# Hybrid two-layer encoder trunk on one core: load order, parameter transfers, first spread and last store

## What is computed

```python
def rms_norm(x, g):
    y = x * lax.rsqrt(jnp.mean(x * x, axis=-1, keepdims=True) + EPS)
    return y * g

x = x + rglru_sgu_mixer(rms_norm(x, norm_ab), w_in_ab, ..., w_out_ab)      # layer 0
#   z = h @ w_in; a_x, a_g, b_u, b_v = split(z, 4)
#   y_a = rg_lru(causal_dwconv(a_x)) * gelu(a_g)
#   y_b = spatial_gating(gelu(b_u), gelu(b_v)); concat(y_a, y_b) @ w_out
x = x + conv_ffn(rms_norm(x, norm_ffn[0]), ...)
x = x + chunk_band_attention(rms_norm(x, norm_attn), w_qkv, rel_bias, w_o)  # layer 1
x = x + conv_ffn(rms_norm(x, norm_ffn[1]), ...)
return rms_norm(x, norm_final)
```

## Time and profile before

| | us |
|---|---|
| median of 3 runs | 1108.13 |
| lowest and highest | 1107.46, 1108.34 |
| the profiled execution | 1108.31 |
| its span, first to last instruction | 1106.4 |
| PE busy in the span | 1094.4 |
| granted TensorE clock, mean | 0.997 |

### The profile page before, as it was taken

The page is one execution under the profiler, slowest core; times in us unless marked ns, Lnnn a source line. Parts: engine busy times, 40 slices in busy tenths (PEclk is TensorE's granted clock), DMA queues, the critical chain, the costliest instruction groups (busy, mean ns, idle before and its releaser), DMA issues.

```text
span 1106.4 us, 15451 instructions
## 1 busy us (share of the span) xinstructions
PE 1094.4 (99%) x5167; PEld 911.4 (82%) x5167; DVE 650.8 (59%) x1068; ACT 436.8 (39%) x672; POOL 530.2 (48%) x415
## 2 busy tenths in 40 slices
PE   8999999999999999999999999999999999999997
PEld 6888888888888888888888888888888888888886
DVE  6777557766666632223877677676766666651113
ACT  6783433322222232334656455453323232233222
POOL 5568645444444445554332323364544444455552
PEclk9999999999999999999999999999999999999998
DMA  8273323222222232333322222132222222223212
GB/s 308 91 240 114 113 78 115 95 95 95 95 95 95 95 114 96 114 108 110 105 92 80 81 91 77 57 114 96 95 100 96 104 98 95 95 95 110 98 39 77
DMA packets 37875, 115.07 MB, mean 104 GB/s; under 512 B 4912, under 2 KB 7600, under 8 KB 37840
## 3 DMA queue, kind: packets, MB, share of 16 engines
q1 hardware_dynamic: 34976, 109.86, 29.6%
q10 hardware_dynamic: 2864, 4.74, 1.3%
HBM read 112.19 MB, written 6.59 MB: 107 GB/s over the span
## 4 chain that ended last, share of the span: by engine, by line
PE 90%; DVE 0%; ACT 0%; DVEq 0%; issue 0%
PE bank L1252 28%; PE bank L1253 28%; PE bank L1254 28%; PE bank L1560 2%; PE bank L1543 2%; PE bank L1572 1%; PE bank L1570 1%; PE bank L1466 0%; PE bank L1465 0%; PE bank L1554 0%; DVE x L1245 0%; PE bank L1291 0%; PE bank L1298 0%; PE bank L1512 0%; PE bank L1504 0%; PE bank L1520 0%
## 5 line engine op out<-in xcount | busy, mean ns | idle before, releaser
L381 POOL TENSOR_TENSOR wl<-raw,wh 128x512 fp32r<-128x512 f32 x190 | 250.1, 1316 | 546.3 <-ACT wh L477 546.3
L1252 PE MATMUL bank<-xh,wh 128*128 128x512 f32 x976 | 382.7, 392 | 2.3 <-DVE xl L859 2.3
L1254 PE MATMUL bank<-xh,wl 128*128 128x512 f32 x976 | 380.2, 390 | 0.0
L1253 PE MATMUL bank<-xl,wh 128*128 128x512 f32 x976 | 380.1, 389 | 0.0
L477 ACT ACTIVATE wh<-raw 128x1024 fp32r<-128x1024 f32 x190 | 201.1, 1061 | 356.0 <-PE bank L1254 313.4
L383 POOL TENSOR_TENSOR wl<-raw,wh 128x512 fp32r<-128x512 f32 x190 | 259.5, 1366 | 0.0
L1252 PEld LDWEIGHTS bank<-xh,wh 128*128 128x128 f32 x976 | 183.2, 188 | 41.8 <-issue 2.1
L1254 PEld LDWEIGHTS bank<-xh,wl 128*128 128x128 f32 x976 | 183.2, 188 | 38.4
L1253 PEld LDWEIGHTS bank<-xl,wh 128*128 128x128 f32 x976 | 183.3, 188 | 36.9
L1252 PE MATMUL bank<-ah,wh 128*128 128x512 f32 (+1 forms) x357 | 134.6, 377 | 0.0
L1253 PE MATMUL bank<-al,wh 128*128 128x512 f32 (+1 forms) x357 | 134.4, 377 | 0.0
(11 more groups left out here) (208 smaller groups left out, 1148.2 us busy)
## 6 DMA issues: line engine op xcount, KB each, us to landing
raw<-weights SPq DMA_DIRECT2D x190, 512.0 KB, 3.2
bias_scratch<-ext_scratch SPq DMA_DIRECT2D x1, 4096.0 KB, 18.2
bias<-bias_scratch ACTq DMA_DIRECT2D x8, 512.0 KB, 3.6
x<-x_in SPq DMA_DIRECT2D x8, 256.0 KB, 5.8
out<-x SPq DMA_DIRECT2D x4, 384.0 KB, 2.9
raw<-weights SPq DMA_DIRECT2D x4, 256.0 KB, 5.7
out<-x ACTq DMA_DIRECT2D x2, 256.0 KB, 2.8
lng<-ln_g SPq DMA_DIRECT2D x1, 256.0 KB, 8.5
```

Source lines behind the costliest of these rows:

```text
L381: nc.gpsimd.tensor_tensor(low[:, 0:FIRST], raw[:, c % RAW, 0:FIRST], high[:, 0:FIRST], ALU.subtract).then_inc(w_half, 1)
L1252: nc.tensor.matmul(dst, w_hi_part, m_hi, start=first, stop=False)
L1253: nc.tensor.matmul(dst, w_hi_part, m_lo, start=False, stop=False)
L1254: return nc.tensor.matmul(dst, w_lo_part, m_hi, start=False, stop=last)
```

## The change

Six things are changed.

1. SP no longer issues the gains. The recurrence's parameters are moved to stand behind the gains, and ACT issues both in one transfer (`par[:, 0:C_FFN]`, now 72 columns, semaphore `gains_in`). DVE's first step on `lam` and ACT's first `xh` wait for it.
2. SP issues x tile 0 first, then the first half of unit 0, x tiles 1 to 3, the second half, x tiles 4 and 5, and then as before. ACT takes x tile 0, first half, x tiles 1 to 3, second half, x tiles 4 and 5, and then as before.
3. ACT's table load for Sqrt moves from in front of the first half to behind the split of unit 4, in front of the root.
4. POOL makes the low parts of the second halves of units 0 and 1 in two pieces of 128x256 also. PE waits for the first piece before k 4, and for the second before k 6.
5. PE does k 0 of unit 3 before `spread_rstd(0)`, with its wait for the unit's low part in front.
6. SP's last store of three tiles is cut into one of two tiles and one of one tile.

```diff
+OUT_PARTS = [[(2, 5), (5, 8)], [(2, 5), (5, 7), (7, 8)]]
+C_LRU = C_GAIN + N_NORMS * KT
+C_FFN = C_LRU + MT_A * 8
...
-            sp.dma_start(par[:, 0:C_FFN], params[:, 0:C_FFN]).then_inc(gains_in, 16)
...
+            load_x(0)
             load_half(0, 0)
-            for m in range(3):
+            for m in range(1, 4):
                 load_x(m)
             load_half(0, 1)
-            for m in range(3, 6):
+            for m in range(4, 6):
                 load_x(m)
...
-                for n in range(2):
-                    tiles_out = slice(OUT_POOL + 3 * n, OUT_POOL + 3 * n + 3)
-                    sp.wait_ge(out_dve, 6 * half + 3 * n + 3)
+                for first, last in OUT_PARTS[half]:
+                    tiles_out = slice(first, last)
+                    sp.wait_ge(out_dve, (KT - OUT_POOL) * half + last - OUT_POOL)
                     sp.dma_start(out[:, tiles_out, cols], x[:, tiles_out, cols]).then_inc(out_done, 16)
...
                 pool.wait_ge(w_hi, c + 1)
-                nc.gpsimd.tensor_tensor(low[:, FIRST:], raw[:, c, FIRST:], high[:, FIRST:], ALU.subtract
-                                        ).then_inc(w_lo, 1)
+                for n, part in enumerate((slice(FIRST, FIRST + FIRST // 2), slice(FIRST + FIRST // 2, UNIT))):
+                    nc.gpsimd.tensor_tensor(low[:, part], raw[:, c, part], high[:, part], ALU.subtract
+                                            ).then_inc(w_lo if n else half_lo, 1)
...
-            act.dma_start(par[:, C_LRU:], params[:, C_LRU:]).then_inc(lru_in, 16)
+            act.dma_start(par[:, 0:C_FFN], params[:, 0:C_FFN]).then_inc(gains_in, 16)
...
-            preload(ACT.Sqrt, 1)
+            act.wait_ge(gains_in, 16)
+            first_hi(0)
             half_hi_part(0)
...
             split_hi(3)
             split_hi(4)
+            preload(ACT.Sqrt, 1)
             statistics(0)
...
+            pe.wait_ge(w_lo, U_AX + 4)
+            tiles(bank[MIX_BANKS[3]][:], U_AX + 3, range(1), True, False, (xh, xl))
             spread_rstd(0)
-            whole(U_AX + 3, MIX_BANKS[3])
+            tiles(bank[MIX_BANKS[3]][:], U_AX + 3, range(1, KT), False, True, (xh, xl)).then_inc(w_used, 1)
```

More of the change, by code:

```diff
@@ L59 @@
 OUT_POOL = 2
-C_FFN = C_GAIN + N_NORMS * KT
+OUT_PARTS = [[(2, 5), (5, 8)], [(2, 5), (5, 7), (7, 8)]]
+C_LRU = C_GAIN + N_NORMS * KT
+C_FFN = C_LRU + MT_A * 8
 FFN_COLS = FF_KT * 8
-C_LRU = C_FFN + 2 * FFN_COLS
-N_PARAMS = C_LRU + MT_A * 8
+N_PARAMS = C_FFN + 2 * FFN_COLS
 EXT = T + P
@@ L229, in trunk @@
         half_in = [sem(f"half_in{i}") for i in range(2)]
-        half_hi, half_lo, warm_ready, lru_in = (sem(n) for n in ("half_hi", "half_lo", "warm_ready", "lru_in"))
+        half_hi, half_lo, warm_ready = (sem(n) for n in ("half_hi", "half_lo", "warm_ready"))
         gains_in, lam_series, rate_done = sem("gains_in"), sem("lam_series"), sem("rate_done")
@@ L331, in _ @@
             load_unit(2)
-            sp.dma_start(par[:, C_FFN:C_LRU], params[:, C_FFN:C_LRU]).then_inc(par_in, 16)
+            sp.dma_start(par[:, C_FFN:], params[:, C_FFN:]).then_inc(par_in, 16)
             for c in range(3, RAW):
@@ L361, in _ @@
                 cols = slice(HALF * half, HALF * half + HALF)
-                for n in range(2):
-                    tiles_out = slice(OUT_POOL + 3 * n, OUT_POOL + 3 * n + 3)
-                    sp.wait_ge(out_dve, 6 * half + 3 * n + 3)
+                for first, last in OUT_PARTS[half]:
+                    tiles_out = slice(first, last)
+                    sp.wait_ge(out_dve, (KT - OUT_POOL) * half + last - OUT_POOL)
                     sp.dma_start(out[:, tiles_out, cols], x[:, tiles_out, cols]).then_inc(out_done, 16)
-            sp.wait_ge(out_done, 16 * 6)
+            sp.wait_ge(out_done, 16 * 7)
         @block.gpsimd
@@ L532, in _ @@
             nc.scalar.activation(ln_tmp, ln_var, ACT.Exp, scale=-1.0).then_inc(lam_exp, 1)
-            preload(ACT.Sqrt, 1)
+            act.wait_ge(gains_in, 16)
+            first_hi(0)
             half_hi_part(0)
-            act.wait_ge(gains_in, 16)
-            for m in range(3):
+            for m in range(1, 4):
                 first_hi(m)
             other_half_hi(0)
-            for m in range(3, 6):
+            for m in range(4, 6):
                 first_hi(m)
@@ L896, in _ @@
             num, den, ratio2, series = ln_tmp, ln_rstd, ln_var, bank[LAM_BANK][:, 0:4]
-            dve.wait_ge(lru_in, 16)
+            dve.wait_ge(gains_in, 16)
             link(ts(lru_rate, lam, -1.0, None, ALU.mult))
@@ L1307, in _ @@
             for unit, k in FIRST_TILES:
-                if k in (0, 2):
-                    pe.wait_ge(half_lo, 2 * unit + 1 + k // 2)
-                if k == FIRST // P:
+                if k in (0, 2, 4):
+                    pe.wait_ge(half_lo, 3 * unit + 1 + k // 2)
+                if k == 6:
                     pe.wait_ge(w_lo, unit + 1)
@@ L1697, in pack_params @@
     cols = [n.reshape(KT, P).T for n in norms]
+    lru = np.concatenate([lru_conv_w, lru_conv_b[None], r_b[None], i_b[None], lam[None]], 0)
+    cols.append(lru.reshape(8, MT_A, P).transpose(2, 1, 0).reshape(P, 8 * MT_A))
     for layer in range(2):
@@ L1704, in pack_params @@
         cols += [tail, np.zeros((P, 4), tail.dtype)]
-    lru = np.concatenate([lru_conv_w, lru_conv_b[None], r_b[None], i_b[None], lam[None]], 0)
-    cols.append(lru.reshape(8, MT_A, P).transpose(2, 1, 0).reshape(P, 8 * MT_A))
     return np.concatenate(cols, 1)
```

## The result

The changed kernel takes 1109.50 us (median of 21 runs, 1108.36 to 1110.72), the kernel before 1108.19 (21 runs, 1107.46 to 1109.11). The ratio is 1.0013, 95% interval 1.0007 to 1.0018: 1.3 us slower. That is less than the 0.2% taken as the bound of "no change", but the interval leaves 1 out, and the time lies outside the range that was forecast (1107.2 to 1108.9). The profiled execution of the changed kernel took 1108.96 us, its span is 1107.0; it is among the quicker ones of the 21.

The account below looks back on a forecast made before the run. PE, busy 1094.4 of 1106.4 us, was taken as the bound. Opening and gates +0.1 and store 0 took 1108.31 to 1108.4 for the profiled execution, less 0.18 over the median: 1108.2 us, range 1107.2 to 1108.9.

Parts of the forecast that it names:

- The step that failed: ACT's parameter transfer in the opening: first `lam` step perhaps 0.1 us later, series ending at 6.14, only tile 0's `xl` delayed.
- The queue's gain: SP's loads in the opening: without the gains ahead, each place lands 0.45 us sooner, x tile 0 at 3.8.
- rival 3: Opening loads land when they did, the lead is -0.25 and the gates come 0.55 late: 1108.7 us, chance 0.08.
- The first product: PE's first product in the opening: starts at 7.75 us, before 8.12.
- the lead of 0.2 us: PE at the end of the opening: unit 1 k 0 starts at 13.2, where it was 13.39.
- unit 1 k 0 behind 13.6: Sign in PE's opening that the forecast is wrong: slower overlap of DVE and POOL, or loads landing no sooner.
- DVE beside POOL: Overlapping ops in the opening: the one starting second loses 0.6 (DVE) or 0.75 (POOL) of the overlap, the first nothing.
- Rival 2: DVE and POOL serialise in the opening: unit 1 k 0 at 14.4, `rstd` 1.3 later, 1109.4 us, chance 0.10.
- The later spread and the gates: Spread without a wait but 0.1 us later; PE then waits 0.6 us for unit 6's low part, gates 0.1 later.
- The table load and the store: Sqrt's load fits ACT's idle time ahead of the root, nothing gained or lost; splitting the last store gives 0.
- Rivals 1 and 4: First: PE's lead is carried on, 1107.6 us, chance 0.22. Second: the store's last part lands sooner, 1107.6, chance 0.10.
- The sum: Whole kernel: opening and gates +0.1 us, store 0, giving 1108.2 us; chance 0.50.

Follow-up runs that it names:

- a_par_on_sp: Changed kernel with the one transfer of 72 parameter columns issued by SP ahead of x tile 0, not by ACT: 1108.57 us.
- b_par_act: Kernel before with all 72 parameter columns in one transfer on ScalarE's queue, SP starting with unit 0's first half: 1109.74 us.
- c_best: Changed kernel with two parts taken back, parameters issued by SP ahead of x tile 0 and the spread before unit 3: 1108.70 us.
- b_spread: Kernel before with one product of unit 3 put ahead of the spread (recurrence's parameters also stand behind the gains): 1108.73 us.
- b_store: Kernel before with only the last store in two parts (recurrence's parameters also stand behind the gains): 1108.10 us.
- a_spread_back: Changed kernel with the spread standing before unit 3 again: 1108.94 us.
- c_hold: Changed kernel with SP issuing parameters first, spread before unit 3, and POOL holding unit 4's low part until `col_done`: 1108.04 us.
- a_hold: Changed kernel with POOL holding unit 4's low part until the column of `rstd` is done (`col_done`): 1109.69 us.
- a_lru_alone: Changed kernel with ACT's parameter transfer cut in two on the same queue, the 16 KB for the `lam` series first: 1109.70 us.
- a_warm20: Changed kernel with 20 warm-up matmuls for 14: median 1109.32 us.

## Why the prediction was wrong, point by point

**The step that failed** is one sentence: "ACT's transfer now has 72 columns for 32, which may put the first `lam` step 0.1 us later; the series behind it ends at 6.14". It was 1.9 us later (4.83 for 2.89), and the series ended at 8.08. Nor did it delay only the `xl` of tile 0: all eight stood behind it. I costed the transfer by its size and didn't ask what starts beside it. Before, both first issues were small; the change put 256 KB at 0.75 us beside it. The trace of before had the bounds: small ones of 1.8 and 2.0 us, large ones of 3.0 and 4.7. "Lands like the large load beside it" would have been the upper bound of that term. Its price is about 0.9 us of the 1.3 (a_par_on_sp); in the kernel before, with the table load behind it, 1.5 us (b_par_act). With the parameters early, the rest of the change took 1108.57, inside the range that was forecast.

**The queue's gain.** x tile 0 landed at 4.55 and not at 3.8: each place should have landed 0.45 sooner, and the first landed 0.3 later than the first load of before (4.2). The second and third landed at 5.2 and 5.9 and were ahead of their places (6.4 and 7.1), but from the fourth load on each lay within 0.2 us of its place before: this part of rival 3 came true. For the first product it didn't matter, since `xl` waited for the series.

**The first product** came at 8.88, not at 7.75; in the kernels with x tile 0 first and early parameters it came at 7.45 to 7.74, near the forecast. So this step was right, but it rested on the sentence above. The lead behind it was not: in those kernels unit 1 k 0 started at 13.53 to 14.09, where 13.2 was forecast, so the lead of 0.2 us wasn't there even with the parameters in time. The sign "unit 1 k 0 behind 13.6" came true in the changed kernel as well (13.86).

**DVE beside POOL.** I took a loss of 0.6 or 0.75 of the overlap, from two rows. It is not a share. An `xl` that starts more than 0.2 us ahead of the end of POOL's piece ends 0.55 us behind that end, in all seven cases of the two traces (before and after), and in the 51 of the other twelve; a POOL piece of 128x256 ends 0.60 behind the `xl`'s end. In the changed kernel the overlaps are 0.56 to 0.67 us, and the ops last longer than I had them:

```profile
L862 DVE SCALAR_TENSOR_TENSOR xl<-x,par,xh x4: 1112/1218/1226, 10.8 to 14.1; 128x512 fp32r<-128x512 f32 x4
```
```profile
L397 POOL TENSOR_TENSOR wl<-raw,wh x2: 1182/1183/1184, 12.4 to 13.6; 128x256 fp32r<-128x256 f32 x2
```

The two rows I worked from fit this as well: 0.34 of 0.54 is the overlap less 0.20, 0.41 of 0.54 is the overlap less 0.13. An op has 0.13 to 0.2 us in which it doesn't need what the other holds, and all the rest is shut out. Nor does the order of start decide to the hundredth: in c_best an `xl` began at 11.66, 0.02 us ahead of POOL's piece, and took 1.30 us, while the piece kept its 0.74. So the Trainium skill's sentence on the exclusive lock, in the section "SBUF: two separate sides" of the page "SBUF — State Buffer", was the better guide than my share; what it has too much is only the fixed part. Rival 2, built on it, went too far for that reason, and its 14.4 for unit 1 k 0 wasn't reached (13.86, though the first `xl` began at 8.00 and not at 6.2). Its time, 1109.4, is the nearest to the measured 1109.50, but by luck: what made the kernel slow is not in it.

**What I didn't see** is that ops of 0.17 us are held too. The 0.52 and the 1.00 stand in the series that I passed over with "`col_done` is there at 26.3". They are what PE waited 0.37 us for, and they follow where POOL's pieces stand, not where the statistics end. In a_par_on_sp and c_best they lasted longest, 2.62 us for the series, and whatever lead there was came to nothing at the spread.

**The later spread and the gates** were right in kind: no wait at the spread, and a new wait for POOL's low part of unit 6, 0.76 us of the weight load where 0.6 was forecast (0.34 us of PE's matmuls). The chain from `rstd` is as rigid as I took it: 27.90 + 0.60 to 39.84 + 1.28 is 12.62 us, 12.64 before, and DVE's 0.52 us of idle time is still in it.

```profile
27.90 0.60 ACT L510 ACTIVATE rstd<-bank 128x512 f32<-128x512 f32 x1 [2.86 <-PE bank L1301]
```
```profile
36.02 0.69 DVE L928 TENSOR_TENSOR axp<-bank,rstd 128x512 f32<-128x512 f32 x1 [0.52 <-DVE axc L935]
```
```profile
39.84 1.28 POOL L384 TENSOR_TENSOR wl<-raw,wh 128x512 fp32r<-128x512 f32 x1
```

Only the size was off: "0.3 us less the lead" had a lead of 0.2, and the opening gave -0.47. That makes 0.77, where the trace shows `rstd` 0.70 later (27.90 for 27.20). Alone, with no change in the opening, the term is 0.3; b_spread's trace gives 0.25 and its median 0.5.

**The table load and the store** were right: the load moved to 22.00, ahead of a root that came at 24.75, and was waited for by nothing; the store gave 0. PE's wait of 0.2 us near the end of the mixer stayed 0.2. Rivals 1 and 4 fell.

**The sum.** In the two profiled executions the gates start 0.68 us later, and the times differ by 0.65 (1108.96 for 1108.31), so all of that difference is in the opening. The medians differ by 1.3, because this profiled run is one of the quicker ones. The other profiles say the same of the place: against before, the third matmul of the gates (41.10) comes between 0.47 us sooner (b_store) and 1.4 later (a_spread_back), and the span differs by the same to 0.13 us in all but b_spread and a_spread_back, which lose 0.5 and 0.3 us more, most of it in the last 11 us. So the time of a run is all but settled at 41 us. What moves it there between runs of one kernel isn't: only one run of each was profiled. Before and b_store, with one order of loads, had x tile 0 at 6.38 and at 5.71 and the gates 0.47 us apart, which speaks for the arrivals of the loads; no run shows it.

## What to carry to other kernels

A small transfer of many packets costs what it starts beside, not what it weighs: issue the ones that a long chain hangs on ahead of the first large load, and on the same queue if need be. Before DVE work is brought forward, look at what POOL does at the new time: with the two sharing SBUF, even an op of 0.17 us can take 1.3 (b_spread's first of the series). Letting POOL wait for the short series gave 0.66 us where PE stood behind it (c_hold), 0.24 within the noise in the kernel before, and nothing where PE had other work (a_hold). And where the chain behind a step has no slack, moving that step behind more PE work fills PE's wait now and gives it back, with the delay on top, where that chain ends.

## What the runs showed of the hardware

- A transfer of 16 KB issued on ScalarE's queue at 0.75 us landed after 2.0 us beside one of 20 KB and after 3.9 us beside one of 256 KB; 36 KB took 3.6 to 4.4 us there, and 1.8 to 1.9 us ahead of the large loads on SP's queue. Its 144 packets went in 0.6 us beside small ones (before) and needed over 2 us beside large ones, with 16 KB (a_lru_alone) as with 36 (the changed kernel).
- DVE's ops with operands in SBUF that began while POOL's subtraction over SBUF still had more than 0.2 us to run ended a fixed time behind POOL's end: 0.55 us for the `xl` (128x512), 0.02 to 0.03 us for 128x4. Not all ops are held: the `RECIPROCAL` that starts beside POOL's op in before and in c_best takes its usual 0.18 us, and the steps of the `lam` series, with an operand in PSUM, their 0.17 beside POOL's pieces.
- The rise of the clock from 1.2 to 2.4 GHz scatters: the warm-up matmuls took 0.63 us each up to 4.2 us and 0.39 soon after it in some profiles (b_store, a_warm20), while the one that started at 7.2 us still took 0.63 in another (b_spread), though PE does the same warm-up in all of them up to there. In one profile (a_spread_back) the clock fell while PE stood for 2.5 us, and the products behind it ran at 1.2 GHz (granted clock 0.50) until 12 us.
- How much later or sooner than before the gates start at 41 us is, to 0.13 us, how much longer or shorter the whole span of 1106 us is, in 11 of 13 kernels profiled beside it.
- A last store of 128 KB behind a full stream landed 3.2 us after its issue, no sooner than one of 384 KB.
